# Three U slots and eight V slots in the expert stage of a hybrid decoder block, with dense V blocks by halves, the ids spread by ScalarE and the dense merge moved to the end

## The chip, the core and the metric

The kernel runs on one core of a Trainium2 chip, as one program and one launch. The metric is the device time of an execution in microseconds, lower is better. Three runs of the kernel before took 2561.82, 2562.2 and 2563.57 us, median 2562.2. One further execution was profiled; all rows below are of it.

## The reference, cut to what matters

One decoder layer over 256 tokens of width 2048: an input projection, sparse attention and a Mamba-2 mixer side by side, an output projection, and then a PEER layer (product-key expert retrieval). The change touches only the PEER layer:

```python
def peer_ffn(h, w_peer_q, peer_keys, peer_u, peer_v):
    q = (h @ w_peer_q).reshape(b, s, 8, 2, 128)              # 8 heads, 2 half keys
    sc = jnp.einsum('bshcd,hckd->bshck', q, peer_keys)
    s1, i1 = lax.top_k(sc[..., 0, :], 16)
    s2, i2 = lax.top_k(sc[..., 1, :], 16)
    cand_s, cand_i = s1 + s2, i1 * 128 + i2                  # all 16 x 16 pairs
    top_s, pos = lax.top_k(cand_s, 16)                       # 16 experts a head and token
    eid, gate = take(cand_i, pos), softmax(top_s)
    act = gelu(einsum('bthkd,btd->bthk', peer_u[eid], h))    # rows of U, 2048 wide
    return einsum('bthk,bthkd->btd', gate * act, peer_v[eid])
```

There are 16384 experts, and each token picks 8 x 16 = 128 of them; U and V are float32, so a row is 8 KB. x plus this result is the output.

## The kernel before, in words

The first 1.3 ms are the projections, the attention and the Mamba mixer. They are not touched, except that the PEER layer begins beside the last projection (w_peer_q).

**Units.** The PEER layer is cut in 16 units: unit u is token tile u // 8 (128 tokens on the partitions) and head u % 8. A unit has 16 picks, and for each pick one gather of U and one of V: an indirect DMA issued by GpSimd (POOL; line 836 for U, line 860 for V) that fetches one row of 8 KB for each of the 128 tokens. There are 256 gathers of U, numbered by dot, and 256 of V. Ids in the last 32 blocks of 128 experts are skipped by the bounds check of the gather; these experts are computed densely by TensorE.

**Slots.** The gathered U rows land in a ring of U_RING = 4 slots of 8 KB a partition (u_slots), the V rows in a ring of V_RING = 7 (v_slots). The last unit's first V gathers go to the U slots, which the dots have left by then.

**Engines in the stage.** VectorE (DVE) makes the dot products of U with h (line 1769, one instruction for one gather), and in units 1 to 7 also the top-16 searches for two later units, in pieces between pairs of dots (top_experts). ScalarE (ACT) makes the gelu of a unit's 16 dots, DVE the weights (weights_of), and TensorE (PE) multiplies groups of four V slots with the weights in four column groups (line 2453). PE goes in periods: period 4u + q is quarter q of unit u, four V gathers, and then the work put beside it: dense U blocks in periods 1 to 27 (PE transposes, ACT copies to u_t, PE multiplies), the one-hot gate matrices in periods 28 to 35 (line 2402), and the 32 dense V blocks in periods 36 to 57 (line 2414). These go one, two, one, two blocks to a period (v_before). A dense V block is 1 MB in one of two dense_raw slots, and 16 matmuls: two token tiles times four banks, eight products in all, two records each.

**Order of the gathers.** POOL's queue is written out by hand and is strictly in order: V gather n comes after U gather n + 19, and from there they alternate one by one. Before a U gather POOL waits for the dot that frees its slot, before a V gather for the PE group that frees its slot (four V slots at once for nearly the whole stage, two at once at the end). SP's queue loads the dense blocks, each when the block before the last has been used.

**Weights and their order.** The weights of unit u are made by DVE after the fourth dot of unit u + 1, so PE's unit u begins after dot 16u + 19.

**Ids for V.** The V gathers need the ids turned among groups of 32 partitions: v_eid. Sixteen small copies do that for a unit. ACT does it for units 0 and 1; DVE for the other 14, 32 copies in one run after the two units' ids are known (line 1756). The semaphore v_ids counts the units done, and POOL waits for it before a unit's first V gather.

**Merges.** The first token tile's sparse sums are added to x when its eight units are done (merge_first, dot 149). Its dense sums are added by merge_dense, right after dot 250 (line 1808), and wait for the last dense V block. The second tile's sums are added at the very end, quarter by quarter (merge_last, line 1886).

```python
U_AT, PICKS_AT, CHUNKS_AT, DENSE_V_AT = 1, 27, 28, 36
MERGE_DOT, GATE_DOT, WEIGH_DOT, LAST_MERGE_DOT = 149, 132, 135, 250
```

Of the kernel before, what the change touches and what calls it, by code (L numbers as in the profile page):

```python
# [6 lines left out]
ACT = mybir.ActivationFunctionType  # L7
# [7 lines left out]
P = 128  # L15
BANK = 512
PIECE_KC = 2
RING = 4
AHEAD = RING - 1
U_RING = 4  # L20
V_RING = 7
GROUP = 32
DENSE = 32
DENSE_HEAD = 16
# [43 lines left out]
def hybrid_block(nc, x, g_norm1, w_in, g_cq, g_ckv, w_uq, w_ukv, g_qn, g_kn, w_iq, w_o_attn,  # L68
# [22 lines left out]
    PK = 16  # L91
# [43 lines left out]
    def sb(name, shape, dtype=F32):  # L135
        size = 4
        for s in shape[1:]:
            size *= s
        t = nc.alloc_sbuf_tensor_at(name, shape, dtype, offset=top[0])
        top[0] += (size + 31) // 32 * 32  # L140
        most[0] = max(most[0], top[0])
        return t
# [159 lines left out]
    top[0] = r_sc_first  # L302
    dense_tail = sb("dense_tail", [P, DENSE_TAIL, T])
    assert top[0] <= r_sc_first + 2 * PH * NK * 4
    top[0] = r_act + (U_RING + V_RING) * 4 * D
    dense_last = sb("dense_last", [P, DENSE - DENSE_HEAD - DENSE_TAIL, T])
    assert top[0] <= r_after_bc
    dense_parts = ((dense_head, 0), (dense_tail, DENSE_HEAD), (dense_last, DENSE_HEAD + DENSE_TAIL))

    def dense_a(b, tokens):  # L310
# [34 lines left out]

    top[0] = r_act
    u_slots = sb("u_slots", [P, U_RING, D])
    r_v = top[0]
    v_slots = sb("v_slots", [P, V_RING, D])
    assert (r_conv - r_v) % (4 * D) == 0  # L350
# [4 lines left out]
    with ExitStack() as ctx:  # L355
# [174 lines left out]

        def v_slot(n):
            if V_IN_U <= n < V_IN_U + U_RING:
                return u_slots[:, n - V_IN_U, :]
            return v_slots[:, v_ring(n) % V_RING, :]

        def v_landing(n):

            if V_IN_U <= n < V_IN_U + U_RING:
                return u_landed[n - V_IN_U], (PK * UNITS // U_RING + 1) * 16
            return v_landed[v_ring(n) % V_RING], (v_ring(n) // V_RING + 1) * 16  # L540

        U_TURNS = D // (TURN * P)
        CHUNKS = T // CHUNK
        HOTS = CHUNK // HOT
        U_AT, PICKS_AT, CHUNKS_AT, DENSE_V_AT = 1, 27, 28, 36
        MERGE_DOT, GATE_DOT, WEIGH_DOT, LAST_MERGE_DOT = 149, 132, 135, 250
        CHUNKS_EACH = 2
        assert CHUNKS_EACH * HOTS == HOT_RING

        def u_before(period):  # L550

            n = period - U_AT
            return min(max(n + min(max(n, 0) // 5, 5), 0), DENSE)
# [2 lines left out]

            return range(u_before(period), u_before(period + 1))

        def v_before(period):

            n = max(period - DENSE_V_AT, 0)
            return min(n + n // 2, DENSE)

        def dense_v(period):

            return range(v_before(period), v_before(period + 1))

        assert u_before(PICKS_AT + 1) == DENSE and v_before(58) == DENSE

        def gate_bank(c):  # L570

# [2 lines left out]
        def spread(u):  # L574
            for n in range(4):
                for i in range(4):
                    g = (i + n) % 4
                    lanes, tokens = slice(i * GROUP, (i + 1) * GROUP), slice(g * GROUP, (g + 1) * GROUP)
                    yield v_eid[lanes, u, :, g], eid[tokens, u, 4 * i:4 * i + 4]
# [325 lines left out]
        def _(act):  # L905
# [279 lines left out]
            def spread_ids(u):  # L1185
# [3 lines left out]
                    ins = act.activation(lanes, ids, ACT.Copy)  # L1189
                ins.then_inc(v_ids, 1)  # L1190

            def query_scores(b):

                for t in range(NT):
                    full(U_late + 20 + NT * b + t)
                    act.activation(sc[t][:, 4 * b:4 * b + 4, :].rearrange("p c k -> p (c k)"),
                                   small[:, t, :], ACT.Copy, scale=rstd[:, t:t + 1]).then_inc(small_free_act, 1)
# [64 lines left out]
            def dense_blocks(period):  # L1262
                for b in dense_u(period):
                    dense_block(b)
# [25 lines left out]
            def hots(period):  # L1290

                first = (period - CHUNKS_AT) * CHUNKS_EACH * HOTS
                if 0 <= first < CHUNKS * HOTS:
                    for j in range(first, first + HOT_RING - 1):
                        hot_of(j)
# [14 lines left out]
            for u in range(UNITS):  # L1310
                for q in range(4):
                    if q == 3 and u + 1 < UNITS:
                        unit_gelu(u + 1)
                    if 4 * u + q == PICKS_AT:
                        copy_picks()
                    dense_blocks(4 * u + q)
                    hots(4 * u + q)
                    if q == 1:
                        selected(u + 1)

        @block.vector
        def _(dve):
# [368 lines left out]
            def top_experts(units, between):  # L1691
# [53 lines left out]
                for u in range(n):  # L1745
                    for c in range(2):
# [2 lines left out]
                wait()  # L1749
                dve.scalar_tensor_tensor(eid[:, all_units, :], part[:, 0, 0:n, :], float(NK), part[:, 1, 0:n, :],  # L1750
                                         ALU.mult, ALU.add).then_inc(unit_ids, n)
                if n > 1:
                    dve.wait_ge(unit_ids, units[-1] + 1)
                    for u in units:
                        for lanes, ids in spread(u):
                            ins = dve.tensor_copy(lanes, ids)
                        ins.then_inc(v_ids, 1)

            def some_dots(u, first, n):
                for k in range(first, first + n):  # L1760
# [24 lines left out]
            def weights_of(u):  # L1785

                dve.wait_ge(gelued, u + 1)
                dve.tensor_tensor(share_s[:, u % 2, :, :], gelu_s[:, u % 2, :, :], gm_s[:, u % 2, :, :],
                                  ALU.mult).then_inc(shared, 1)
                if u >= 2:  # L1790
                    dve.wait_ge(v_free, 4 * (u - 1))
                dve.wait_ge(shared, u + 1)
                dve.tensor_tensor(weight[:, u % 2, :, :, :].rearrange("p q g i -> p (q g) i"),
                                  block_ident[:, :].unsqueeze(1).broadcast_to([P, PK, GROUP]),
                                  share_s[:, u % 2, :, :].rearrange("p q g -> p (q g)").unsqueeze(2)
                                  .broadcast_to([P, PK, GROUP]), ALU.mult).then_inc(weighed, 1)
# [14 lines left out]
            def merge_dense():  # L1811

                dve.wait_ge(dense_used, DENSE)
                dve.wait_ge(merged, 2)
                add_first()
# [47 lines left out]
            def after_dot(i):  # L1863

                n = i - GATE_DOT
                if n >= 0 and n % 2 == 0 and n // 2 < CHUNKS:
                    if n == 0:
                        dve.wait_ge(iota_ready, 2)
                    gates_of(n // 2)
                n = i - GATE_DOT - 2  # L1870
                if n >= 0 and n % 4 == 0 and n // 4 < CHUNKS // CHUNKS_EACH:
                    last_hot_of(n + HOT_RING - 1)
                n = i - WEIGH_DOT
                if n >= 0 and n % 2 == 0 and n // 2 < CHUNKS:
                    weigh_dense(n // 2)
                if i == MERGE_DOT:
                    merge_first()
                if i == LAST_MERGE_DOT:
                    merge_dense()

            def merge_last():

                for c in range(4):
                    dve.wait_ge(summed, c + 1)
                    cols = x1_back[:, 1, c * BANK:(c + 1) * BANK]
                    dve.tensor_tensor(cols, cols, (small, pair_d)[c // 2][:, c % 2, :], ALU.add).then_inc(merged, 1)
# [56 lines left out]
            for u in range(1, UNITS):  # L1943
# [17 lines left out]
                        picks_of()  # L1961
                some_dots(u, dotted[0], PK - dotted[0])
            weights_of(UNITS - 1)
            merge_last()


        @block.tensor
        def _(pe):
# [434 lines left out]
                                        hot_gate[:, c % 2, n, :], start=True, stop=True)  # L2403
                    ins.then_inc(hot_used, 1)

            def dense_sums(i):

                if i == 0:
                    pe.wait_ge(a_ready, len(dense_parts) * CHUNKS)
                pe.wait_ge(dense_landed[i % 2], (DENSE // 2 + i // 2 + 1) * 16)  # L2410
                for t in range(NT):
                    for c in range(4):
                        ps = ((A, B), (small, pair_d))[t][c // 2]
                        ins = pe.matmul(ps[:, c % 2, :], dense_a(i, slice(t * P, (t + 1) * P)),
                                        dense_raw[:, i % 2, c * BANK:(c + 1) * BANK],
                                        start=t == 0 and i == 0, stop=t == 0 and i == DENSE - 1, skip_group_check=True)
                ins.then_inc(dense_used, 1)

            def beside(period):

                if period == 0:
                    pe.wait_ge(h2_ready, NT)
                    for r in range(KC // 2):
                        turn_h2(r)
                    pe.wait_ge(h2_copied, KC // 2)
                if period == PICKS_AT:
                    turn_picks()
                    pe.wait_ge(picks_back, 2)
                for b in dense_u(period):
                    dense_dots(b)  # L2430
                for c in range(CHUNKS_EACH * (period - CHUNKS_AT), CHUNKS_EACH * (period - CHUNKS_AT + 1)):
                    if 0 <= c < CHUNKS:
                        dense_gates(c)
                for i in dense_v(period):
                    dense_sums(i)

            pe.wait_ge(small_free_act, sf_act_l + 4 + 4 * NT)
            for u in range(UNITS):
# [50 lines left out]
```

## Time and profile before

| | |
|---|---|
| median of three runs | 2562.2 us |
| profiled execution | 2566.43 us, of which its span 2564.8 us |
| PE busy | 2235.6 us (87%) |
| DVE busy | 1696.0 us (66%) |
| ACT busy | 994.6 us (39%) |
| POOL busy | 899.4 us (35%) |
| HBM read | 840.30 MB |
| gathers (POOL's queue) | 410.47 MB |

Times of a stage are read from the stage's own windows, since these shares are means over stages with different limits. A DMA's time "to landing" is counted from the start of the instruction that issues it.

### The profile page before, as it was taken

Reading aid. Unit: us, or ns where it says so; the run is one execution under the profiler, and the core shown is the slowest. Engines: PE = TensorE matmul, PEld = TensorE weight load, DVE = VectorE, ACT = ScalarE, POOL = GpSimd, SP = SyncE. Lnnn points to the kernel's source line nnn. Section 1 sums busy time; section 2 is a strip of 40 time slices with the busy share of each in tenths; the row PEclk is TensorE's granted clock in tenths of the full one; section 3 lists DMA queues with packets and bytes.
Section 4 is the critical chain, followed back from the end, with each engine's and each line's share of the span. In section 5 each row is a group of like instructions: output and inputs, shape, how many; then the busy total and the mean of one; then the engine's idle time right before and its main releaser. Section 6 shows DMA issues by size and latency. Waiting matters only on the chain.

```text
span 2564.8 us, 35790 instructions
## 1 busy us (share of the span) xinstructions
PE 2235.6 (87%) x12351; PEld 1668.4 (65%) x12351; DVE 1696.0 (66%) x2796; ACT 994.6 (39%) x1900; POOL 899.4 (35%) x632
## 2 busy tenths in 40 slices
PE   7999999999999999999994687788888876776876
PEld 6899888888888888878992355465556532222321
DVE  5888647767766767775686877678777854444442
ACT  4465545545545545545443232233337700111000
POOL 1400011000000100130036666666677764655654
PEclk9999999999999999999997798898996688988888
DMA  5444456665655665646689999999999999999997
GB/s 175 135 148 148 159 179 184 195 190 168 197 188 166 199 188 166 198 155 238 210 288 370 337 405 388 382 392 398 380 374 382 359 393 383 393 385 399 370 387 275
DMA packets 221249, 707.05 MB, mean 276 GB/s; under 512 B 37034, under 2 KB 72226, under 8 KB 162082
## 3 DMA queue, kind: packets, MB, share of 16 engines
q0 software_dynamic: 75584, 410.47, 41.1%
q1 hardware_dynamic: 145056, 294.92, 34.9%
q8 instruction: 63, 1.03, 0.2%
q14 instruction: 50, 0.41, 0.0%
q10 hardware_dynamic: 496, 0.23, 0.0%
HBM read 840.30 MB, written 4.26 MB: 329 GB/s over the span
## 4 chain that ended last, share of the span: by engine, by line
PE 62%; DMA 19%; DVE 6%; issue 6%; POOL 5%; ACT 2%; POOLq 0%; DVEq 0%; ACTq 0%
DMA v_slots<-in_peer_v_dram,v_eid 13%; DMA u_slots<-in_peer_u_dram,eid 6%; PE accA L1992 5%; PE accA L1994 5%; PE accA L1993 4%; PE accB L1992 4%; PE accB L1994 4%; PE accB L1993 4%; PE pair_d L2366 3%; PE accB L1986 2%; PE accB L1984 2%; PE accB L1985 2%; PE small L2453 2%; POOL u_slots L836 2%; PE small L2002 2%
## 5 line engine op out<-in xcount | busy, mean ns | idle before, releaser
L1769 DVE CUSTOM_DVE_ANT_0 dot_junk<-u_slots,h 128x2048 bf16<-128x2048 f32 x240 | 549.7, 2290 | 331.0 <-DMA u_slots<-in_peer_u_dram,eid 325.9
L1330 DVE TENSOR_TENSOR w_lo<-w_raw,w_hi 128x1024 fp32r<-128x1024 f32 (+1 forms) x409 | 508.2, 1252 | 281.6 <-ACT w_hi L913 280.2
L913 ACT ACTIVATE w_hi<-w_raw 128x1024 fp32r<-128x1024 f32 (+1 forms) x420 | 442.1, 1056 | 405.8 <-PE accB L1994 121.5
L836 POOL DMA_INDIRECT u_slots<-in_peer_u_dram,eid x256 | 376.9, 1472 | 306.0 <-DVE dots L1769 190.5
L860 POOL DMA_INDIRECT v_slots<-in_peer_v_dram,v_eid x252 | 388.9, 1543 | 228.0 <-PE pair_d L2453 81.9
L2366 PE MATMUL pair_d<-h_t,u_t 128*128 128x256 f32 x1024 | 244.2, 387 | 14.9 <-ACT u_t L1258 14.9
L1237 ACT ACTIVATE gelu_s<-dots 32x4 f32<-32x4 f32 x256 | 52.9, 207 | 448.8 <-DVE dots L1769 445.9
L2453 PE MATMUL small<-v_slots,weight 128*32 128x512 f32 x496 | 97.5, 845 | 142.1 <-DMA v_slots<-in_peer_v_dram,v_eid 138.8
L2366 PEld LDWEIGHTS pair_d<-h_t,u_t 128*128 128x128 f32 x1024 | 189.6, 193 | 44.9 <-ACT u_t L1258 22.5
L2453 PE MATMUL accA<-v_slots,weight 128*32 128x512 f32 x512 | 89.8, 835 | 127.6 <-DMA v_slots<-in_peer_v_dram,v_eid 110.1
L1258 ACT ACTIVATE u_t<-small 128x512 f32<-128x512 f32 x128 | 72.9, 596 | 289.9 <-PE small L2002 289.6
L805 POOL TENSOR_TENSOR y_skip<-x_tok,per_head_g 128x512 f32<-128x512 f32 x16 | 24.2, 1528 | 424.0 <-ACT x_tok L1141 424.0
L1992 PE MATMUL accA<-w_hi,act_hi 128*128 128x512 f32 x352 | 142.0, 403 | 7.1 <-DVE w_lo L1330 3.6
L2453 PEld LDWEIGHTS small<-v_slots,weight 128*32 128x32 f32 x496 | 19.4, 136 | 197.2 <-issue 197.2
L1984 PE MATMUL accB<-act_hi,w_hi 128*128 128x256 f32 x512 | 145.2, 284 | 1.9 <-ACT ya L1094 1.1
L1985 PE MATMUL accB<-act_lo,w_hi 128*128 128x256 f32 x512 | 144.9, 283 | 0.0
L1986 PE MATMUL accB<-act_hi,w_lo 128*128 128x256 f32 x512 | 144.9, 283 | 0.0
L1994 PE MATMUL accA<-w_hi,act_lo 128*128 128x512 f32 x352 | 139.2, 396 | 0.0
L1993 PE MATMUL accA<-w_lo,act_hi 128*128 128x512 f32 x352 | 138.7, 394 | 0.0
L1992 PE MATMUL accB<-w_hi,act_hi 128*128 128x512 f32 (+1 forms) x352 | 137.6, 391 | 0.0
L1994 PE MATMUL accB<-w_hi,act_lo 128*128 128x512 f32 (+1 forms) x352 | 135.7, 386 | 0.0
L1993 PE MATMUL accB<-w_lo,act_hi 128*128 128x512 f32 (+1 forms) x352 | 135.6, 385 | 0.0
(457 smaller groups left out, 4780.5 us busy)
## 6 DMA issues: line engine op xcount, KB each, us to landing
w_raw<-in_w_in_dram SPq DMA_DIRECT2D x168, 512.0 KB, 3.8
w_raw<-in_w_in_dram SPq DMA_DIRECT2D x128, 256.0 KB, 3.1
w_raw<-in_w_o_ssm_dram SPq DMA_DIRECT2D x64, 512.0 KB, 4.4
dense_raw<-in_peer_u_dram SPq DMA_DIRECT2D x32, 1024.0 KB, 8.9
dense_raw<-in_peer_v_dram SPq DMA_DIRECT2D x32, 1024.0 KB, 9.0
w_raw<-in_w_o_attn_dram SPq DMA_DIRECT2D x32, 512.0 KB, 4.2
w_raw<-in_w_out_dram SPq DMA_DIRECT2D x32, 512.0 KB, 4.5
w_raw<-in_w_peer_q_dram SPq DMA_DIRECT2D x32, 512.0 KB, 4.7
```

The source lines that it names most:

```text
L836: pool.indirect_dma_start(u_slots[:, n % U_RING, :], None, peer_u[0], bass.IndirectOffsetOnAxis(ap=eid[:, u, k:k + 1], axis=0), bounds_che ...
L860: pool.indirect_dma_start(v_slot(n), None, peer_v[0], bass.IndirectOffsetOnAxis(ap=v_eid[:, u, m // 4, m % 4:m % 4 + 1], axis=0), bounds_c ...
L913: act.activation(w_hi[:, slot, :, 0:w], w_raw[:, slot, :, 0:w], ACT.Copy).then_inc(hi_split, 1)
L1330: dve.tensor_tensor(w_lo[:, slot, :, 0:w], w_raw[:, slot, :, 0:w], w_hi[:, slot, :, 0:w].bitcast(F32), ALU.subtract).then_inc(lo_split, 1)
L1769: dve.tensor_tensor_reduce(dot_junk[:, :] if i >= PK else slot, slot, h2[:, u // PH, :], 1.0, 0.0, ALU.mult, ALU.add, dots[:, u % 2, k:k + ...
L1984: pe.matmul(o, wh, ah, start=start and c % 2 == 0, stop=False, skip_group_check=True)
L1985: pe.matmul(o, wh, al, start=False, stop=False, skip_group_check=True)
L1992: pe.matmul(o, ah, wh, start=start, stop=False)
L1993: pe.matmul(o, ah, wl, start=False, stop=False)
L1994: ins = pe.matmul(o, al, wh, start=False, stop=stop)
L2366: ins = pe.matmul(pair_d[:, 0, b % 2 * T:(b % 2 + 1) * T], u_t[:, n % 2, i * P:(i + 1) * P], h2_t[:, kc, :], start=kc == 0, stop=kc == KC - 1)
L2453: ins = pe.matmul(ps[g * GROUP:(g + 1) * GROUP, c % 2, :], weight[:, u % 2, q, g, :], v_slot(n + g)[:, c * BANK:(c + 1) * BANK], start=h = ...
```

## The change

U_RING goes from 4 to 3 and V_RING from 7 to 8. The eleven slots stay eleven; the 8 KB that held part of the dense activations (dense_last) moves from behind the V slots to the place of the fourth U slot. PE's dense V work is cut by token tile: half a block is the four banks of one token tile, and each of the periods 36 to 56 takes three halves, period 57 the last one. merge_dense moves from dot 250 to the place after the last unit's weights. The ids of units 2 to 15 are copied by ACT instead of DVE, eight copies after the dense work of each of the four periods of units 1 to 7. The expressions for V gathers that land in U slots follow the new ring size.

```diff
-U_RING = 4
-V_RING = 7
+U_RING = 3
+V_RING = 8
...
-    top[0] = r_act + (U_RING + V_RING) * 4 * D
+    top[0] = r_act + U_RING * 4 * D
     dense_last = sb("dense_last", [P, DENSE - DENSE_HEAD - DENSE_TAIL, T])
-    assert top[0] <= r_after_bc
+    assert top[0] <= r_act + 2 * KC * T * 4
...
     u_slots = sb("u_slots", [P, U_RING, D])
+    top[0] = r_act + 2 * KC * T * 4
     r_v = top[0]
...
         def v_slot(n):
             if V_IN_U <= n < V_IN_U + U_RING:
-                return u_slots[:, n - V_IN_U, :]
+                return u_slots[:, (PK * UNITS + n - V_IN_U) % U_RING, :]
...
-        def v_before(period):
-            n = max(period - DENSE_V_AT, 0)
-            return min(n + n // 2, DENSE)
-        def dense_v(period):
-            return range(v_before(period), v_before(period + 1))
+        def v_halves(period):
+            n = 3 * (period - DENSE_V_AT)
+            return range(min(max(n, 0), NT * DENSE), min(max(n + 3, 0), NT * DENSE))
...
+            def spread_part(units, q):
+                per = 16 * len(units) // 4
+                for n in range(per * q, per * (q + 1)):
+                    u = units[n // 16]
+                    if n == 0:
+                        act.wait_ge(unit_ids, units[-1] + 1)
+                    ins = act.activation(*list(spread(u))[n % 16], ACT.Copy)
+                    if n % 16 == 15:
+                        ins.then_inc(v_ids, 1)
...
                     dense_blocks(4 * u + q)
+                    if u and top_units(u):
+                        spread_part(top_units(u), q)
                     hots(4 * u + q)
...
-                if n > 1:
-                    dve.wait_ge(unit_ids, units[-1] + 1)
-                    for u in units:
-                        for lanes, ids in spread(u):
-                            ins = dve.tensor_copy(lanes, ids)
-                        ins.then_inc(v_ids, 1)
...
-                if i == LAST_MERGE_DOT:
-                    merge_dense()
...
             weights_of(UNITS - 1)
+            merge_dense()
             merge_last()
...
-            def dense_sums(i):
-                if i == 0:
-                    pe.wait_ge(a_ready, len(dense_parts) * CHUNKS)
-                pe.wait_ge(dense_landed[i % 2], (DENSE // 2 + i // 2 + 1) * 16)
-                for t in range(NT):
-                    for c in range(4):
+            def dense_sums(i, t):
+                if t == 0:
+                    if i == 0:
+                        pe.wait_ge(a_ready, len(dense_parts) * CHUNKS)
+                    pe.wait_ge(dense_landed[i % 2], (DENSE // 2 + i // 2 + 1) * 16)
+                for c in range(4):
...
-                for i in dense_v(period):
-                    dense_sums(i)
+                for n in v_halves(period):
+                    dense_sums(n // NT, n % NT)
```

## Rows read from the trace of the kernel before

**Rows 1.** Windows: the stages; busy us by engine, clock, DMA share, GB/s

```profile
1290.00:1450.00 160.00, 108.13 (x744) 85.43 (x743) 123.61 (x221) 57.74 (x154) 85.49 (x57) 0.84 0.90 333
1450.00:1900.00 450.00, 362.08 (x2074) 243.75 (x2073) 341.48 (x796) 124.70 (x334) 293.28 (x189) 0.90 0.98 390
1900.00:2060.00 160.00, 137.86 (x869) 99.38 (x868) 126.94 (x167) 112.92 (x338) 120.00 (x72) 0.73 0.96 363
2060.00:2490.00 430.00, 318.43 (x1184) 119.00 (x1187) 202.45 (x185) 33.07 (x160) 244.09 (x174) 0.87 0.97 391
2490.00:2565.00 75.00, 49.11 (x232) 14.55 (x224) 17.38 (x18) 3.31 (x16) 27.95 (x23) 0.85 0.75 276
```

**Rows 2.** Windows of 5 us inside the dense V stage

```profile
2095.00:2100.00 5.00, 5.00 (x13) 2.28 (x12) 3.55 (x3) 0.00 (x0) 4.39 (x3) 1.00 0.90 338
...
2165.00:2170.00 5.00, 0.67 (x4) 0.23 (x8) 2.30 (x2) 0.00 (x0) 1.98 (x2) 0.50 1.01 418
...
2175.00:2180.00 5.00, 5.00 (x15) 2.20 (x12) 2.78 (x3) 0.00 (x0) 3.33 (x2) 1.00 0.60 213
...
2420.00:2425.00 5.00, 5.00 (x13) 2.16 (x12) 2.60 (x4) 0.00 (x0) 4.39 (x3) 1.00 0.79 280
```

**Rows 3.** Waits, 2060 to 2490 us: total us, times, longest

```profile
POOL u_slots L836 <- DVE dots L1769: 70.8, 21, 4.3
POOL v_slots L860 <- PE pair_d L2453: 66.5, 16, 6.3
```

**Rows 4.** Timeline of POOL, then PE, dense V stage: start, us, what

```profile
2214.91 3.09 POOL L860 DMA_INDIRECT v_slots<-in_peer_v_dram,v_eid  x1 [4.87 <-PE pair_d L2453]
...
2209.05 3.25 PE L2453 MATMUL small<-v_slots,weight 128*32 128x512 f32 x16 [9.11 <-DMA v_slots<-in_peer_v_dram,v_eid]
2213.94 1.99 PE L2414 MATMUL accA<-dense_raw,dense_head 128*128 128x512 f32 x4
...
2220.91 1.88 PE L2414 MATMUL accA<-dense_raw,dense_head 128*128 128x512 f32 x4
```

**Rows 5.** Landing times of U gathers, 1450-1900, 1900-2060, 2060-2490 us

```profile
DMA to landing us min/median/max: 7.0/11.9/16.2
...
DMA to landing us min/median/max: 7.2/9.8/14.3
...
DMA to landing us min/median/max: 9.4/14.9/18.3
```

**Rows 6.** Groups by line, 1450-1900 us: DVE's copies; busy us, mean ns, idle before

```profile
L1756 DVE COPY v_eid<-eid 32x4 uint32<-32x4 uint32 x192 | 34.2, 178 | 2.8
```

**Rows 7.** Waits, 1450 to 1900 us

```profile
POOL v_slots L860 <- PE accB L2453: 59.1, 17, 7.6
POOL u_slots L836 <- DVE dots L1769: 41.9, 10, 7.0
```

**Rows 8.** Timeline: one run of copies on DVE, POOL's wait, ACT's copies

```profile
1667.48 6.33 DVE L1756 COPY v_eid<-eid 32x4 uint32<-32x4 uint32 x32
...
1677.01 2.43 POOL L836 DMA_INDIRECT u_slots<-in_peer_u_dram,eid  x1 [4.94 <-DVE dots L1769]
...
1368.70 3.48 ACT L1189 ACTIVATE v_eid<-eid 32x4 uint32<-32x4 uint32 x16
```

**Rows 9.** Timeline, start of the stage: DVE, then POOL

```profile
1299.27 2.29 DVE L1769 CUSTOM_DVE_ANT_0 u_slots<-u_slots,h 128x2048 f32<-128x2048 f32 x1
...
1302.43 1.13 POOL L836 DMA_INDIRECT u_slots<-in_peer_u_dram,eid  x1 [6.54 <-DVE dots L1769]
```

**Rows 10.** Timeline of the end: DVE, POOL, PE

```profile
2500.49 1.22 DVE L1808 TENSOR_TENSOR x_back<-x_back,accA 128x1024 f32<-128x1024 f32 x1 [11.65 <-PE pair_d L2414]
...
2505.92 2.43 POOL L836 DMA_INDIRECT u_slots<-in_peer_u_dram,eid  x1 [10.64 <-DVE dots L1769]
...
2530.59 3.63 PE L2453 MATMUL small<-v_slots,weight 128*32 128x512 f32 x8 [3.90 <-DMA v_slots<-in_peer_v_dram,v_eid]
...
2558.82 0.69 DVE L1886 TENSOR_TENSOR x_back<-x_back,small 128x512 f32<-128x512 f32 x1 [39.15 <-PE small L2453]
```

More of the change, by code:

```diff
@@ L538, in v_landing @@
             if V_IN_U <= n < V_IN_U + U_RING:
-                return u_landed[n - V_IN_U], (PK * UNITS // U_RING + 1) * 16
+                i = PK * UNITS + n - V_IN_U
+                return u_landed[i % U_RING], (i // U_RING + 1) * 16
             return v_landed[v_ring(n) % V_RING], (v_ring(n) // V_RING + 1) * 16
@@ L545, in hybrid_block @@
         U_AT, PICKS_AT, CHUNKS_AT, DENSE_V_AT = 1, 27, 28, 36
-        MERGE_DOT, GATE_DOT, WEIGH_DOT, LAST_MERGE_DOT = 149, 132, 135, 250
+        MERGE_DOT, GATE_DOT, WEIGH_DOT = 149, 132, 135
         CHUNKS_EACH = 2
@@ L557, in dense_u @@
             return range(u_before(period), u_before(period + 1))
-        def v_before(period):
-            n = max(period - DENSE_V_AT, 0)
-            return min(n + n // 2, DENSE)
-        def dense_v(period):
-            return range(v_before(period), v_before(period + 1))
-        assert u_before(PICKS_AT + 1) == DENSE and v_before(58) == DENSE
+        def v_halves(period):
+            n = 3 * (period - DENSE_V_AT)
+            return range(min(max(n, 0), NT * DENSE), min(max(n + 3, 0), NT * DENSE))
+        assert u_before(PICKS_AT + 1) == DENSE and v_halves(58) == v_halves(4 * UNITS)
         def gate_bank(c):
@@ L2404, in dense_gates @@
                     ins.then_inc(hot_used, 1)
-            def dense_sums(i):
-                if i == 0:
-                    pe.wait_ge(a_ready, len(dense_parts) * CHUNKS)
-                pe.wait_ge(dense_landed[i % 2], (DENSE // 2 + i // 2 + 1) * 16)
-                for t in range(NT):
-                    for c in range(4):
[L2413 to L2417, printed above, removed]
+            def dense_sums(i, t):
[4 more added lines that the diff above has]
+                for c in range(4):
+                    ps = ((A, B), (small, pair_d))[t][c // 2]
+                    ins = pe.matmul(ps[:, c % 2, :], dense_a(i, slice(t * P, (t + 1) * P)),
+                                    dense_raw[:, i % 2, c * BANK:(c + 1) * BANK],
+                                    start=t == 0 and i == 0, stop=t == 0 and i == DENSE - 1, skip_group_check=True)
+                if t == NT - 1:
+                    ins.then_inc(dense_used, 1)
             def beside(period):
```

## The prediction

> **What bounds the kernel now.** I looked first at the busy table in slices, to see where the limit changes. Up to 1290 us TensorE is full and DMA half busy; nothing of the change lies there. From about 1350 us on the DMA engines are near full. So I took windows over the stages [rows 1]. The reader is to see that in the early expert stage (1450 to 1900 us) and in the dense V stage (2060 to 2490 us) no engine is at its limit (PE 80% and 74%, DVE 76% and 47%), while the DMA share is 0.98 and 0.97 at 390 and 391 GB/s. Bytes set the time. The question is whether 391 GB/s is all there is. Windows of 5 us in the dense V stage say no [rows 2]: most run near 418 GB/s, and once in some 40 us there is a hole of one to three windows, the deepest 213; there are nine of them, the first at 2095 and the last at 2420. If 418 were held throughout, the stage would be 430 x (1 - 391/418) = 28 us shorter; the early one, at 420, 450 x (1 - 390/420) = 32 us.
>
> Then the waits and POOL's timeline, to see what digs the hole. POOL waits for PE to free V slots (66.5 us, 16 times) and for DVE to free U slots (70.8 us, 21 times) [rows 3]. The long ones look like [rows 4]: PE began its V group at 2209.05 after waiting 9.11 us for a landing, and POOL's V gather came at 2214.91, when that group was through, after POOL had stood 4.87 us. With seven slots and groups of four, the last V gather of a group needs the slot of the group before it, so POOL stands for the whole V group whenever PE has been waiting. The queue runs dry behind that.
>
> **The rings.** With eight slots V gather 4m+3 needs the group before the last, four gathers earlier than it must. PE's group takes 2213.94 - 2209.05 = 4.9 us [rows 4]. POOL has 174 gathers in 430 us [rows 1], half of them of U: one U gather in 430/87 = 4.95 us, so POOL is two or three pairs past gather 4m+3 when it lands; it gets to the next locked gather only about when the group is through. I count the PE waits of POOL in the dense V stage as mostly gone.
>
> The price is the U ring. A U slot is held for the time to landing plus 3.2 us: from 1299.27, the start of a dot, to 1302.43, the gather it lets through [rows 9]. Three slots can therefore pass one gather in (L + 3.2 + w)/3, L the landing time and w how long landed rows wait for DVE. What each stage needs:
> - Dense V stage: today's 4.95 us allow L + w = 11.7, and the 4.65 us at 418 GB/s allow 10.8. Today L is 14.9 [rows 5] with some 2 x 14.9/4.95 = 6 gathers in flight, most of it queueing; DVE is 47% busy there [rows 1], so w is near nothing. With three slots there are 2 x 10.8/4.65 = 4.6 in flight. The gate stage (1900 to 2060 us) has L = 9.8 at 160/36 = 4.4 us a U gather, 4.4 in flight, with a share of 0.96 [rows 1, 5]. So three slots should do.
> - Early stage: 189 gathers, 450/95 = 4.74 us for one of U [rows 1], allow L + w = 11.0 against L = 11.9 today. L falls with the depth, but DVE is 76% busy and w is one to two us. It just does.
> - Gate stage: 4.4 us allow 10.0 against L = 9.8 alone, and DVE is 79% busy, so w is not small. Here three slots are short.
>
> **Values.** Dense V stage, rings and halves together: between 28 us gained (no holes) and 33 lost: the gate stage, the one row at this depth, moves 363 GB/s, and 430 x (391/363 - 1) = 33. That row is the farther one, since PE at 86% and DVE at 79% hold the gate stage back [rows 1] and its traffic has no dense blocks. I take a gain of 12, less than half of what the holes hold, since four and a half in flight are thinner than six. Cutting dense blocks in halves issues the same matmuls; a block takes 2220.91 - 2213.94 = 7.0 us [rows 4], so periods of 7 and 14 us of dense work become 10.5 each, and PE's period of 4.9 + 10.5 = 15.4 us stays under the 18.6 us that DMA needs. It adds no wait: a dense block has a V group and a half block before it is due. It goes into the 12.
>
> Early stage: bounds -20 to +20. The V waits are 59.1 us, 17 times, the U waits 41.9, 10 times [rows 7], and with one fewer U slot part of the first turns into the second. I take -3 together with the copies, below.
>
> Gate stage: from 0 to 0.5 us for each of 36 dots, +18; the loop dot, U gather, V gather, landing, PE group, gates and next weighing takes about 22.5 us for five dots, 4.5 against 4.4 us each (an estimate from the landing of 9.8, the V group of 4.9 and the gate products beside them). I take +3.
>
> Start (1290 to 1450 us): the first dots stand between splits of w_peer_q on DVE. U gather 3 waits for dot 0 instead of going at once, and the last of unit 0 waits for dot 12 instead of 11. The last dot is on the path to the first weights, so they come up to one dot interval later. The closest spacing seen is 3.2 us, from a dot to the gather behind it [rows 9]. I take +3; below it is 0, above it 6, as the split behind a late dot would be late too.
>
> **The ids.** DVE loses 32 copies for each of seven pairs of units, 6.33 us in one run, behind which POOL stood 4.94 us for a U slot [rows 8]; 192 copies fill 34.2 us of the early stage [rows 6]. ACT gets 8 a period at 3.48/16 = 0.22 us, 1.7 us [rows 8]. ACT is 28% busy in the early stage and 71% in the gate stage [rows 1]. Queued behind them are ACT's u_t copies for PE, the hot matrices of periods 28 to 31, and the next gelu. PE waits for a V group in nearly every period, which covers 1.7 us; where the gelu of the next unit is what DVE waits for it costs up to 1.7 us, once in a unit. The ids come later, but unit 2's are ready in period 5, and the V slot that its first gather takes is freed in period 6: no wait for POOL. Of the early stage's -3 this part is -4; the shorter U ring and later gelus are +1. Bounds of this part: -15 (half of the 34.2), and +7 x 1.7 = +12.
>
> A rule of the Trainium skill bears on these copies. The trace shows gathers that take POOL 1.13 us (1302.43 in [rows 9]) and others that take 2.43 (1677.01 in [rows 8]). The Trainium skill, page "SBUF — State Buffer", section on the "DVE blocks DMA" trap, says that a DVE copy of float32 can shut GpSimd out while it writes descriptors; by it taking 224 copies off DVE would free POOL's issue too. DVE stays 47 to 79% busy with dots and other work [rows 1], so I give it nothing.
>
> **The merge.** After dot 250 DVE waited 11.65 us for the last dense block and added for 2.3 us; POOL stood 10.64 us for dot 251 with the last U gather and every remaining V gather behind it [rows 10]. In that hole DMA fell to 0.75 of the last 75 us [rows 1]. Without it the U gather is bound by dot 252, some 4 us a dot later than dot 250: about 2498 instead of 2505.9, and the V gathers follow. V 239, on whose landing PE began its last run at 2530.59 [rows 10], lands 9 to 10 us earlier; from there PE works through at its own pace to the first closing addition at 2558.82. The two additions move into DVE's 39.15 us of waiting [rows 10], and the 1 MB store of the first tile, which used the hole, now runs beside gathers and costs up to 2.5 us of them. Eight V slots let the very last gathers go a pair sooner, 1 us. I take -9; bounds -14 and -2.
>
> **Sum.** +3 - 3 + 3 - 12 - 9 = -18 us on the profiled execution of 2566.4 us, that is 2548. This execution lies 4.2 us over the median of the runs shown, so for the median I forecast 2544.
>
> **Rivals.**
> 1. The rate is already the chip's. 391 GB/s is what mixed traffic gives, the holes are repaid later, and only the merge helps: +3 + 0 + 3 - 9 = -3, about 2559. For it: the share is 0.97. Against it: 418 GB/s in windows of the same traffic [rows 2]. The Trainium skill, page "SBUF — State Buffer", section on the bandwidth-pool intuition, gives some 358 GB/s for HBM to one core; by that rule there would be nothing to fill and this rival would hold. The trace disagrees, with 418.
> 2. Three U slots are too few (the slower side). If L stays at 9.8 in the early stage and w is 2, a gather takes (9.8 + 3.2 + 2)/3 = 5.0 instead of 4.74 us: 95 x 0.26 = 25 us, the gate stage +8, the start +5, the dense V stage -4 and the merge -9: +25, or 2587. It decides from L + w over 11 us in the early stage; at L + w = 12, 0.33 us over, the sum is of that size, at 11.5 it is about +9, 2571. For it: DVE's busy share there [rows 1]. Against it: 11.9 is a queued landing, the least is 7.0 [rows 5].
> 3. The queue runs full everywhere: early -20, dense V -25, the rest as forecast: -48, 2514. For it: both wait sums of POOL shrink together. Against it: the depth falls from six to four and a half.
>
> **Chances.** The forecast 0.5 (2533 to 2555), rival 1 0.16, rival 2 0.2 (2567 to 2587, and a thin part about zero), rival 3 0.14. A measurement tells 0.2% from nothing, 5.1 us. From the cases: faster 0.5 + 0.14 + a third of rival 1 = 0.7, the same 0.11, slower 0.19. The range leaves out the outer ends of rivals 2 and 3: 2518 to 2576. The forecast's own is 2533 to 2555.
>
> **What would show it.** In the trace after: 5 us windows of the dense V stage without values under 350; POOL's waits for PE there under 20 us, and its waits for DVE up, to 100 or more; median landings of 10 to 12 us in place of 14.9; PE's periods about 19.4 us; no DVE row of line 1808 before the last weights and no POOL wait near 10 us at the end; the last 75 us some 9 shorter. It is wrong if DVE's waits for U in the early stage rise with landings no shorter, or if the holes stay with POOL waiting for dots instead.

## The result and the profile after

Three runs and a profiled one of each: the changed kernel takes 2595.3 us (2589.2 to 2595.6), the kernel before 2562.9. The ratio is 1.0127 (95% interval 1.0115 to 1.0139), 32 us slower. The forecast was 2544 us, and even its slow rival ended at 2587. The profiled span went from 2564.8 to 2593.9 us.

Windows over the stages of the kernel after, as in [rows 1] (busy us of PE, PEld, DVE, ACT, POOL with instruction counts, clock, DMA share, GB/s); the later bounds are shifted with the work:

```profile
1290.00:1450.00 160.00, 106.76 (x726) 83.91 (x725) 115.97 (x187) 57.38 (x152) 76.25 (x55) 0.83 0.88 327
1450.00:1900.00 450.00, 352.86 (x2004) 237.16 (x2003) 298.69 (x586) 155.41 (x493) 274.96 (x183) 0.89 0.95 375
1900.00:2090.00 190.00, 153.51 (x966) 109.70 (x963) 138.76 (x187) 129.73 (x405) 128.79 (x78) 0.74 0.91 338
2090.00:2520.00 430.00, 314.13 (x1167) 118.33 (x1168) 198.74 (x182) 33.06 (x160) 233.46 (x171) 0.87 0.98 388
2520.00:2593.00 73.00, 53.87 (x243) 15.78 (x241) 21.34 (x22) 3.31 (x16) 36.74 (x28) 0.88 0.87 327
```

The early stage (1450 to 1900 us) moves 375 GB/s where [rows 1] had 390, with DVE 43 us less busy (34.2 us of it the copies [rows 6]) and ACT 31 us more. The gate stage stands at 338. The dense V stage (2090 to 2520 us) has the share and the rate of before. In the last 73 us the DMA share is higher (0.87 against 0.75).

POOL's and DVE's waits, kernel after, at 1450 to 1900 us and then at 2090 to 2520 us (total us, times, longest):

```profile
POOL u_slots L834 <- DVE dots L1774: 112.8, 28, 14.2
...
POOL u_slots L834 <- PE accB L2458: 9.8, 4, 4.5
...
DVE dot_junk L1774 <- DMA u_slots<-in_peer_u_dram,eid: 130.8, 61, 5.8
...
POOL u_slots L834 <- DVE dots L1774: 131.0, 37, 5.4
...
POOL u_slots L834 <- PE pair_d L2458: 15.0, 4, 4.6
```

Against [rows 7] (59.1 us for PE, 41.9 for dots) and [rows 3] (66.5 and 70.8) the waits for V slots are nearly gone, as forecast, and those for dots have grown by more. DVE in turn waits for landings 61 times in the early stage; in the kernel before it was

```profile
DVE dot_junk L1769 <- DMA u_slots<-in_peer_u_dram,eid: 81.9, 43, 4.9
```

POOL waits for the dot, the dot for a landing, and the landing for POOL: that looks like a ring of slots which sets the pace; the limit of three below tests it. Landings of U gathers in the kernel after, 1450 to 1900 and 2090 to 2520 us:

```profile
DMA to landing us min/median/max: 6.3/10.0/15.0
...
DMA to landing us min/median/max: 7.8/12.0/15.8
```

They fell from 11.9 and 14.9 [rows 5]. In the early stage that is not enough: the stage takes longer all the same.

To see where the 29 us arise I took the start of each unit's first dot from DVE's timeline of several kernels, less that of the kernel before:

```
us behind the kernel before      unit 1   unit 4   unit 8   unit 11  unit 15  last dot
after                              5.4      0.4     16.5     36.5     36.3     29.5
rings 3/8 alone                    4.4      9.3     27.5     41.9     39.7     44.9
three in flight, units 1-7        -1.8      6.1     26.5     29.9     28.3     29.0
three in flight, units 8-10       -2.3     -7.4     -6.0      8.0      5.6      5.6
ids on ACT alone                  -1.6    -12.9     -9.6      0.3     -1.5     -1.1
merge alone                       -4.4     -5.8     -6.0     -5.5     -7.8    -14.0
merge alone, again                 1.0     -2.0     -3.7     -1.4     -2.9     -9.3
V limited to six                   0.6      5.9     35.3     44.7     57.7     59.3
```

In the kernel after: start +5, units 1 to 7 +11, units 8 to 10 +20, units 11 to 14 nothing, tail -7. Two profiles of one kernel (the merge alone) lie 5 us apart by unit 1, so a difference under some 6 us here says little by itself. The +5 at the start stands in all four kernels with three U slots (4.4 to 5.4), and in none with four (-4.4 to 1.0).

### The profile page after: what moved, and what is told of

It is laid out like the page before. It is cut to its first block, busy times and chain, and to the rows that moved or that the text cites. A ratio compares the mean times of both kernels' runs of the same rounds, so it can differ in the third digit from the quotient of the medians.

```text
span 2593.9 us, 35791 instructions
## 1 busy us (share of the span) xinstructions
PE 2240.7 (86%) x12351; PEld 1670.4 (64%) x12351; DVE 1657.5 (64%) x2572; ACT 1041.3 (40%) x2124; POOL 878.9 (34%) x632
## 4 chain that ended last, share of the span: by engine, by line
PE 50%; DMA 24%; DVE 8%; issue 8%; POOL 7%; ACT 2%; POOLq 0%; DVEq 0%; ACTq 0%; SPq 0%
DMA u_slots<-in_peer_u_dram,eid 18%; DMA v_slots<-in_peer_v_dram,v_eid 5%; PE accA L1996 4%; PE accA L1998 4%; PE accA L1997 4%; PE accB L1996 4%; PE accB L1998 4%; PE accB L1997 4%; POOL v_slots L858 4%; POOL u_slots L834 4%; DVE dot_junk L1774 4%; PE accB L1990 2%; PE accB L1988 2%; PE accB L1989 2%; PE small L2006 2%
## 5 line engine op out<-in xcount | busy, mean ns | idle before, releaser
L834 POOL DMA_INDIRECT u_slots<-in_peer_u_dram,eid x256 | 331.0, 1293 | 490.3 <-DVE dots L1774 349.5
L858 POOL DMA_INDIRECT v_slots<-in_peer_v_dram,v_eid x253 | 414.2, 1637 | 91.2 <-issue 79.2
L2458 PE MATMUL accA<-v_slots,weight 128*32 128x512 f32 x512 | 95.1, 881 | 138.0 <-DMA v_slots<-in_peer_v_dram,v_eid 118.3
L2458 PEld LDWEIGHTS accA<-v_slots,weight 128*32 128x32 f32 x512 | 19.3, 140 | 180.8 <-issue 180.8
```

What stands on the lines that cost most here:

```text
L834: pool.indirect_dma_start(u_slots[:, n % U_RING, :], None, peer_u[0], bass.IndirectOffsetOnAxis(ap=eid[:, u, k:k + 1], axis=0), bounds_che ...
L858: pool.indirect_dma_start(v_slot(n), None, peer_v[0], bass.IndirectOffsetOnAxis(ap=v_eid[:, u, m // 4, m % 4:m % 4 + 1], axis=0), bounds_c ...
L2458: ins = pe.matmul(ps[g * GROUP:(g + 1) * GROUP, c % 2, :], weight[:, u % 2, q, g, :], v_slot(n + g)[:, c * BANK:(c + 1) * BANK], start=h = ...
```

## The experiments

All are edits of the kernel before, where nothing else is said. The first seven split the change, the others test the reasons.

**Rings of three and eight alone; rings of three and seven alone.**

```diff
-U_RING = 4
-V_RING = 7
+U_RING = 3
+V_RING = 8
```

(V_RING stays 7 in the second; the moved dense_last goes with both.)

> The kernel before with the rings alone changed (3 U and 8 V slots). Theory A, three U slots hold the gathers back: most of the 32 us loss is here, less what the merge gives back, so +25 to +40 us against before (2588 to 2603), units 4 to 10 longer, POOL's waits for dots above 250 us in all. Theory B, the ids on ACT are the loss and the rings are neutral or a gain: 2545 to 2568.

> The kernel before with one U slot fewer and nothing given for it (3 and 7). Theory A: the U ring alone decides once it has three slots; the eighth V slot is idle capacity, so the same as 3 and 8 within 5 us. Rival: the eighth V slot does repay something in the dense V stage, and this one is 10 us or more slower than 3 and 8.

Measured 2606.6 us, ratio 1.0165 (1.0143 to 1.0186), and 2608.3 us, 1.0182 (1.0164 to 1.02). One U slot fewer costs 42 to 47 us, a little over the 25 to 40 expected, and the eighth V slot gives back nothing that can be told from zero. The windows of 3/8 alone, 1450 to 1900, 1900 to 2090 and 2090 to 2520 us:

```profile
1450.00:1900.00 450.00, 349.12 (x2002) 234.79 (x2000) 327.50 (x745) 122.26 (x332) 265.23 (x183) 0.89 0.96 374
1900.00:2090.00 190.00, 143.03 (x905) 99.75 (x907) 141.93 (x213) 118.96 (x349) 117.11 (x77) 0.74 0.90 337
2090.00:2520.00 430.00, 324.61 (x1252) 126.93 (x1244) 202.70 (x189) 33.84 (x164) 241.50 (x171) 0.88 0.98 390
```

The same rates as after, 375, 338 and 388: the loss of the change is that of its U ring.

**The ids on ACT alone; the merge at the end alone; halves alone.** Each is its part of the change's diff and no more.

> The kernel before with the ids of units 2 to 15 copied by ACT in quarters and nothing else. Theory B: the copies stand before the hot matrices and the gelus and cost 5 to 20 us, most of it about period 28 (2568 to 2583). Theory A: DVE's 6.3 us runs go, ACT has room, 0 to 6 us faster (2557 to 2563).

> The kernel before with the dense merge moved to the end and nothing else. Both theories: 7 to 11 us faster (2552 to 2556), since POOL's 10.6 us stop at dot 251 goes. Rival: the store of the first tile and the last gathers share the time, and no more than 3 us are left.

> The kernel before with dense V blocks by halves and nothing else. If the holes of 40 us rhythm come from the two-block periods: 5 to 15 us faster (2548 to 2558), unit times 11 to 14 down from 81 to 78. If they come from POOL standing behind each V group and from POOL's slow issue: 0 to 3 us either way.

Measured: ids 2564.5 us, 1.0008 (0.9998 to 1.0019), nothing. Merge 2552.7 us, 0.996 (0.9944 to 0.9976). Halves 2557.4 us, 0.9981 (0.9967 to 0.9996), about 5 us, but not where the theory put it: units 11 to 14 took 325.5 us in its profile against 325.0 before. The ids are not inert: the table has them 13 us ahead by unit 4 and level by unit 11.

**The three with the old rings; the kernel after with its ids back on DVE.**

> The changed kernel with the old rings (4 and 7): ids, merge and halves as changed. Theory A: all of the loss and more goes, 2548 to 2558, faster than before. Theory B: 2565 or more, since the ids are still on ACT.

> The changed kernel with the ids of units 2 to 15 back on DVE. Theory A: the 6.3 us runs now stand before three slots instead of four and hurt more, 2595 to 2610. Theory B: the loss of the gate stage goes, 2570 to 2582.

Measured 2559.8 us, 0.9992 (0.9972 to 1.0011), and 2599.2 us, 1.0134 (1.0105 to 1.0163) against 1.0127 for the kernel after. With the old rings the whole loss is gone, though the kernel does not come out 4 us or more ahead (2548 to 2558), as the theory asked; with the new ones no difference by the ids can be told. Inside the change the rings cost some 34 us (1.0127 against 0.9992), less than alone: the parts don't simply add.

**Merge and halves together, old rings, ids on DVE.**

> The kernel before with its rings of four and seven and its ids on VectorE, and two parts of the change: the dense merge at the end and the dense V work by halves. If the gains of the two parts add up (merge -10 us, halves -5 us when each stood alone), about 2548 us, a ratio of 0.994. If the halves are worth nothing once the tail is short, as in the kernel that had merge, halves and ids together (2559.8), 2552 to 2554. It also says what the ids cost inside that kernel: with the sum of -15 here the ids would take some 10 us of it.

Measured 2554.6 us, 0.9971 (0.996 to 0.9983). No better than the merge alone: the gains don't add.

**At most three U gathers in flight, four slots in memory.** Dots 16 to 127 in one kernel, 128 to 175 in the other:

```diff
                 if n >= U_RING:
-                    pool.wait_ge(u_free, n - U_RING + 1)
+                    pool.wait_ge(u_free, n - (U_RING - 1 if 16 <= n < 128 else U_RING) + 1)
```

> The kernel before, four U slots in memory, but the gathers of dots 16 to 127 (units 1 to 7) wait for the dot three back, as with three slots. Theory (a slot is held for at least 14.6 us, from issue to issue, so three of them pass one gather in 4.9 us instead of 4.77): units 1 to 7 get 15 to 20 us longer, and the gate stage can't give it back: ratio about 1.006 to 1.008, 2578 to 2582 us. Rival (bytes set the time, a late start of the gate stage is repaid by emptier queues): under 8 us, 1.000 to 1.003.

> The same, with the limit of three on the gathers of dots 128 to 175 alone (units 8 to 10, the gate stage and the end of the first dense V periods). Theory: units 8 to 10 get 10 to 15 us longer (14.4 in the kernel with the rings alone), all of it kept: ratio 1.004 to 1.006, 2573 to 2578 us. Rival (in that stage TensorE and VectorE set the pace and the queue depth doesn't matter): within 0.1% of before, and then the 14 us came from being late out of the early stage.

Measured 2587.6 us, 1.0094 (1.0072 to 1.0116), and 2573.4 us, 1.005 (1.0034 to 1.0067). Both losses stay to the end: units 1 to 7 took 28 us more in the first, units 8 to 10 took 14 more in the second. The profiled execution of the first is 7 us slower than its median; by the ratio the loss is 24 us (18 to 30), not under the 15 to 20 of the theory, so the rival (a late start is repaid) falls. POOL's waits of the first at 1450 to 1900 us:

```profile
POOL u_slots L836 <- DVE dots L1769: 121.7, 32, 9.6
```

No slot was taken away and no V slot added, and the row is that of the kernel after (112.8 us, 28 times).

The ring can be read from the timelines of POOL and DVE. For each U gather k I took the time from its issue to its dot, and from that dot to the issue of gather k+3; their sum is how long one of three slots is held:

```
mean us                     issue to dot  dot to k+3's issue  sum/3   spacing of U issues
units 1-7   before (four)       12.9            -               -          4.67
            after               10.7           3.78            4.83        4.82
            rings 3/8 alone     10.9           3.81            4.90        4.87
            limit of three      11.0           3.86            4.95        4.90
units 8-10  before (four)       13.2            -               -          4.62
            rings 3/8 alone     10.7           3.92            4.87        4.92
            limit of three      10.6           3.87            4.82        4.85
units 11-14 before (four)       15.1            -               -          5.08
            after               11.9           3.36            5.09        5.09
            rings 3/8 alone     11.8           3.36            5.05        5.08
```

In units 1 to 10 a third of the hold is more than the 4.6 to 4.7 us at which four slots run. In units 11 to 14 the spacing is 5.08 with either ring, and the gathers just land sooner.

**Five U slots and six V slots; V limited to six.** From U gather 48 on (FIVE_AT) the U ring takes over one V slot (the slots, landings and releases of all gathers are worked out ahead). In the other kernel the slots stay and the V gathers wait as if there were six:

```diff
+            if (kind, n) == ("u", FIVE_AT):
+                rings["u"].insert(0, rings["v"].pop(0))
...
-                    pool.wait_ge(v_free, v_freed(v_ring(n) - V_RING))
+                    pool.wait_ge(v_free, v_freed(v_ring(n) - V_RING + (1 if n >= 32 else 0)))
```

> The kernel before with five U slots and six V slots from U gather 48 on: the U ring takes over one V slot there. Theory (with four slots a U gather is held 19 us against a floor of 14.6, so slots are no longer the bound, bytes are): a fifth slot gains nothing, 0 to -4 us, and six V slots cost 0 to 8, as the last two V gathers of each group now wait for the group before: ratio 0.999 to 1.003. Rival (each slot more is worth its share of the 42 us that the fourth brought): 10 us or more faster, under 0.996.

> The kernel before with four U and seven V slots in memory, but from V gather 32 on each waits for the PE group that held the slot six gathers back, as with six V slots. Theory (the whole loss of the kernel with five and six is the V ring: the last two gathers of each group of four wait for the group before, and the U gathers stand behind them): ratio about 1.025 to 1.03, 2625 to 2640 us. Rival (six V slots cost 10 to 30 us, and the rest came from the fifth U slot, whose gathers crowd out V's landings on which PE waits): 1.004 to 1.012.

Measured 2635.7 us, 1.0291 (1.0256 to 1.0326), and 2624.4 us, 1.0232 (1.0217 to 1.0248). Both theories of the first missed by far: one had -4 to +8 us, the other 10 us or more gained, and it was +75. The second, whose limit begins at about the same gather (V 32 against 29), says that 62 us of this are the V ring. Up to the last dot the two lose the same (57 and 59 us), so nothing shows that the fifth U slot repays any of it; the profiled span of five and six is 7 us longer, lost behind the last dot, where POOL stood 16.54 us for PE among the last V gathers. POOL's waits in the second kernel, 1450 to 1900 us, and two gathers of its timeline:

```profile
POOL v_slots L860 <- PE accB L2453: 107.8, 17, 10.2
...
POOL u_slots L836 <- DVE dots L1769: 8.6, 2, 4.4
...
1712.36 0.99 POOL L836 DMA_INDIRECT u_slots<-in_peer_u_dram,eid  x1 [0.30 <-issue]
1720.87 0.99 POOL L860 DMA_INDIRECT v_slots<-in_peer_v_dram,v_eid  x1 [7.52 <-PE accB L2453]
1722.17 3.06 POOL L836 DMA_INDIRECT u_slots<-in_peer_u_dram,eid  x1 [0.30 <-issue]
```

As many waits for PE as in [rows 7], 17, and each nearly twice as long (6.3 us against 3.5). While POOL stands, no U gather goes either: the one at 1722.17 had its slot free and went 0.30 us after the V gather. So while the V ring is locked a free fifth U slot is of no use.

**The merge with ids on ACT for units 2 to 13 only; the merge alone, again.** The last pair's ids stay on DVE, with a semaphore of their own:

```diff
-                if n > 1:
+                if UNITS - 1 in units:
...
-                        ins.then_inc(v_ids, 1)
+                        ins.then_inc(last_ids, 1)
...
+                    if 0 < u < 7:
+                        spread_part(top_units(u), q)
```

> The kernel before with the merge at the end and the ids of units 2 to 13 copied by ScalarE in quarters, those of units 14 and 15 by VectorE as before, so that no ScalarE copy stands in periods 28 to 31 ahead of the hot matrices. Theory (the copies in these periods are what gave the gain back): the 8 to 12 us gained by unit 4 are kept, on top of the merge's 10: ratio 0.992 to 0.994, 2541 to 2546 us. Rival (the gain is given back because the bytes or PE catch up in the gate stage whatever ScalarE does): as the merge alone, 0.996, 2552.

> The merge at the end alone, once more, on the same chip as the kernel with merge and ids. Expected 0.996 again, 2552 us, -10.

Measured 2554.6 us, 0.9965 (0.9953 to 0.9977), and 2556.3 us, 0.998 (0.9969 to 0.9991). The theory asked for 0.994 or less, so ACT's copies ahead of the hot matrices are not all of the giving back. The collision is there to see in the kernel after (timelines of ACT, PE, DVE and POOL at the start of the gate stage):

```profile
1942.18 3.50 ACT L1197 ACTIVATE v_eid<-eid 32x4 uint32<-32x4 uint32 x16
1945.68 2.44 ACT L1292 ACTIVATE hot<-iota_k,pick_t 128x128 f32<-128x128 f32 x8
...
1949.45 14.04 PE L2406 MATMUL small<-hot_gate,hot 128*128 128x32 f32 x64 [4.11 <-ACT hot L1296]
...
1956.61 0.42 DVE L1866 TENSOR_TENSOR dense_head<-dense_head,small 128x256 f32<-128x256 f32 x1 [10.18 <-PE small L2406]
...
1960.51 1.32 POOL L834 DMA_INDIRECT u_slots<-in_peer_u_dram,eid  x1 [10.64 <-DVE dots L1774]
```

Copies, matrices, PE's gates, DVE's additions, the next dot, POOL: one chain. But units 8 to 10 took 9.9 us more with all ids on ACT (table: -9.6 to 0.3) and still 4.6 more without those of the last pair, and that kernel had lost 6 us of its early gain (14.0 us at unit 4) before the gate stage. What takes that back is open.

The merge alone (twice), merge with halves, and merge with these ids are all faster than the kernel before by 6 to 10 us, and their intervals overlap; none is shown to be the best. All of them beat the changed kernel by 39 us or more.

## Why the prediction was wrong

**The U ring is the step that failed: "three slots should do", "It just does", and in the gate stage "I take +3".** The formula was right and so was the rival's direction; the term that was mis-sized is the 3.2 us from a dot to the gather it lets through. It came from one row at the start of the stage [rows 9], and it was quoted as the closest spacing seen; the mean over units 1 to 7 is 3.8. (L is the time to landing, w the wait of a landed row for DVE.) With issue to dot at 10.9 (L + w, forecast to be allowed 11.0, so this part held) the hold is 14.7 us and a third of it 4.90, against 4.67 before. 112 gathers times 0.20 to 0.23 (by the spacing measured, 4.87, or the third of the hold) are 22 to 26 us; the rings alone lost 23 in these units. With 3.2 in place of 3.8 the same sum gives 4.70 and 3 us: this term makes nearly all of the difference. In the gate stage 14.6 / 3 = 4.87 against 4.62 makes 12 us for 48 gathers, and 14 were lost. I had compared with 4.4 us there, had seen that "three slots are short", and still took +3 of bounds of 0 and 18. The limit of three, applied to each stage by itself, showed both sums and that nothing repays them.

Where the extra 0.6 us come from can be counted. In the kernel after units 1 to 7 have 112 dots, and the gather that each lets through comes in one of three ways. 41 times it came some 3.16 us after the dot's start: POOL stood waiting. 43 times it took some 3.46: POOL was issuing a V gather, which ended 0.87 us after the dot, and the U gather followed 0.30 us later. 28 times it took 4.7 us or more, 5.1 in the mean: POOL was a pair behind. With the rings alone the three counts are 44, 38 and 30. One case of each; DVE's timeline and then POOL's, kernel after:

```profile
1700.74 2.28 DVE L1774 CUSTOM_DVE_ANT_0 dot_junk<-u_slots,h 128x2048 bf16<-128x2048 f32 x1
...
1703.17 2.29 DVE L1774 CUSTOM_DVE_ANT_0 dot_junk<-u_slots,h 128x2048 bf16<-128x2048 f32 x1
...
1719.53 2.28 DVE L1774 CUSTOM_DVE_ANT_0 dot_junk<-u_slots,h 128x2048 bf16<-128x2048 f32 x1
...
1728.23 2.29 DVE L1774 CUSTOM_DVE_ANT_0 dot_junk<-u_slots,h 128x2048 bf16<-128x2048 f32 x1
...
1703.90 2.43 POOL L834 DMA_INDIRECT u_slots<-in_peer_u_dram,eid  x1 [4.52 <-DVE dots L1774]
1706.64 0.99 POOL L858 DMA_INDIRECT v_slots<-in_peer_v_dram,v_eid  x1 [0.30 <-issue]
1707.93 2.67 POOL L834 DMA_INDIRECT u_slots<-in_peer_u_dram,eid  x1 [0.30 <-issue]
...
1722.69 0.99 POOL L834 DMA_INDIRECT u_slots<-in_peer_u_dram,eid  x1 [3.02 <-DVE dots L1774]
1723.98 0.99 POOL L858 DMA_INDIRECT v_slots<-in_peer_v_dram,v_eid  x1 [0.30 <-issue]
...
1728.62 2.77 POOL L858 DMA_INDIRECT v_slots<-in_peer_v_dram,v_eid  x1 [0.30 <-issue]
1731.70 0.99 POOL L834 DMA_INDIRECT u_slots<-in_peer_u_dram,eid  x1 [0.30 <-issue]
```

The dot at 1719.53 let a waiting POOL go at 1722.69, 3.16 us later. The dot at 1728.23 found POOL about to issue a V gather, which took 2.77 us beside it, and the next U gather went 3.47 us after the dot's start. The dot at 1703.17 came close behind the one at 1700.74. It stretched the U gather that the first one had let through (2.43 us from 1703.90), a V gather came behind that, and its own U gather went only at 1707.93, 4.76 us after its start. Such cases carry most of the term: of the 63 us by which the 112 exceed 3.2 us each, the 28 have 53. A strict queue adds such pieces, and the shortest row shows none of them.

**The eighth V slot.** Its step, POOL's waits for PE gone, came true (15.0 us in 4 waits against 66.5 in 16). The time did not follow, since the waits turned into waits for dots. Beside four U slots an eighth V slot was not tried; it doesn't fit in memory. Six V slots cost 62 us, so of the splits that ran four and seven is the best.

**Dense V stage, -12: measured 0.** Units 11 to 14 took 325.0 us before, 324.8 after, 322.8 with the rings alone, 322.6 with three in flight before them. In all kernels but those with six V slots they took 322.0 to 325.5 us, 5.03 to 5.09 us a dot, whatever their rings, halves or ids. Rival 1 was right for this stage: it gets 388 to 391 GB/s with either pair of rings, and the windows near 418 were held in neither kernel. That the DMA itself sets this pace fits its share of 0.97 to 0.98 but is argued: no run took bytes away from the stage. Windows of 5 us after, and POOL's timeline ahead of the first two:

```profile
2230.00:2235.00 5.00, 5.00 (x22) 2.01 (x15) 2.58 (x4) 4.43 (x22) 3.37 (x2) 1.00 0.87 321
2235.00:2240.00 5.00, 5.00 (x13) 2.15 (x12) 2.45 (x3) 2.18 (x11) 4.20 (x3) 1.00 0.87 308
...
2390.00:2395.00 5.00, 5.00 (x27) 1.49 (x20) 2.92 (x3) 2.58 (x13) 4.09 (x4) 0.72 0.77 256
...
2470.00:2475.00 5.00, 5.00 (x28) 1.12 (x20) 2.61 (x3) 1.94 (x10) 2.05 (x3) 0.53 1.02 415
...
2225.15 0.99 POOL L834 DMA_INDIRECT u_slots<-in_peer_u_dram,eid  x1 [5.41 <-DVE dots L1774]
```

The prediction had named this sign against itself: the holes stay, with POOL waiting for dots. Here it stood 5.41 us for one, 5 us ahead of the hole at 2230.

**Halves.** Alone they measured -1 to -8 us, beside the merge nothing.

**The ids, -4: measured 0** over the kernel. The gain is real in the early stage and is given back by unit 11, perhaps in part through the queue of ACT that the prediction named; what else takes it back is open.

**The start, +3:** +4 to +5. **The merge, -9:** right. After dot 250 nothing stops, the additions stand in DVE's wait as forecast, and the tail is 7 us shorter; alone it gave 10 and 6 us in two measurements. DVE's last rows after:

```profile
2549.15 1.22 DVE L1813 TENSOR_TENSOR x_back<-x_back,accA 128x1024 f32<-128x1024 f32 x1
2550.28 1.22 DVE L1813 TENSOR_TENSOR x_back<-x_back,accB 128x1024 f32<-128x1024 f32 x1
2587.87 0.69 DVE L1889 TENSOR_TENSOR x_back<-x_back,small 128x512 f32<-128x512 f32 x1 [36.38 <-PE small L2458]
```

**The chances.** Rival 2, three U slots are too few, had the right direction and 0.2. That its 25 us for the early stage lie near the 23 measured is luck in part: it counted L + w = 11.8 with 3.2 behind it, and measured were 10.9 with 3.8. By its own sign, L + w over 11, it would have been dismissed. Its end of 2587 also counted a gain of 4 in the dense V stage and only +8 for the gates, and its value at L + w = 11.5 is too low by its own formula: (11.5 + 3.2)/3 = 4.90, 95 x 0.16 = 15 us, not 9. With the terms measured on the rings alone and the merge alone the sum reads +5 + 23 + 14 + 0 - 6 to -10 = +32 to +36, against 32; the halves and the ids are near nothing in it. In the changed kernel the same loss lies otherwise: +11 in units 1 to 7, where the ids on ACT gained, and +20 in units 8 to 10, where they gave it back (with the ids back on DVE it is +24 and +15).

## What to carry to other kernels

A ring of slots passes one transfer in (issue to use + use to next issue) / slots; take both terms as means over the stage to be changed, not from the shortest row, since two tenths of a microsecond times a hundred gathers is the whole effect. Where two rings are fed by one queue in strict order, a free slot in one is worth nothing while the other is locked, so neither can be shortened to lengthen the other unless its hold leaves room. And before counting holes in the transfer rate as gain, see whether the stage's pace moves at all when queue depth does.

## What the runs showed of the hardware

With the ring cut from four to three the median landing of a U gather fell only from 11.9 to 10.0 us in the early stage, and from 14.9 to 12.0 in the dense V stage, where the rate stayed (391 and 388 GB/s): there the fourth slot only lengthened the time to landing. And a gather that POOL begins to issue while a dot runs ends some 0.87 us after the dot's end: the V gather of 1728.62 ended at 1731.39, the dot at 1730.52. So it was with 151 of 159 such gathers in the kernel after and 178 of 180 before; the others began within 0.05 us of the dot's start and took 0.99 us, as most gathers beside no dot do. It is not only the dots: the gather of 1302.43 [rows 9] took 1.13 us and ended 0.86 us after a tensor_tensor of DVE (w_lo from w_raw and w_hi, 1301.48 to 1302.70). The Trainium skill tells, in "SBUF — State Buffer" on the "DVE blocks DMA" trap, of such a hold-up behind a DVE copy of float32. The trace has the hold-up, but behind dots and tensor_tensor, which read two inputs. The copies, for which the prediction weighed the trap, last 0.18 us each and show none: the 17 gathers that POOL began during one of them in the kernel before took 0.99 us each, and 224 copies fewer on DVE did not change the time.
